# A decoder trunk: state tiles worked on in pairs, with 32-row products in alternate row groups

## The reference

```python
bu_r = jnp.einsum('bsgc,gpc->bsgp', ug, bb_r)      # 16 groups, 16 channels -> 64 states
bu_i = jnp.einsum('bsgc,gpc->bsgp', ug, bb_i)
_, _, h_r, h_i = lax.associative_scan(_cplx_combine, (a_r, a_i, bu_r, bu_i), axis=1)
y = (jnp.einsum('bsgp,gcp->bsgc', h_r, c_re) - jnp.einsum('bsgp,gcp->bsgc', h_i, c_im)
     + d.reshape(SSM_GROUPS, SSM_CH) * ug)
```

## Time and profile before

| | us |
|---|---|
| median of 3 runs | 1702.06 (1700.05 to 1702.82) |
| profiled execution, its own time | 1703.64 |
| span of that execution | 1701.5 |
| PE busy | 1655.4 (97%) |
| DVE busy | 1356.3 (80%) |
| ACT busy | 1084.3 (64%) |
| POOL busy | 225.5 (13%) |

### The profile page before, as it was taken

One profiled execution on the slowest core, in us unless ns is written; L12 is line 12 of the kernel. 1 busy time (PEld: TensorE's weight loads), 2 busy tenths in 40 slices (PEclk: granted clock), 3 DMA queues, 4 the chain that ended last, 5 costly groups with the idle time before them and its releaser, 6 DMA issues.

```text
span 1701.5 us, 24284 instructions
## 1 busy us (share of the span) xinstructions
PE 1655.4 (97%) x8488; PEld 1384.4 (81%) x8488; DVE 1356.3 (80%) x1519; ACT 1084.3 (64%) x1202; POOL 225.5 (13%) x236
## 2 busy tenths in 40 slices
PE   7899999999999999899999999999999999999997
PEld 7778888888897889788888888888888888888785
DVE  6986656555678765679988988988988989889897
ACT  5355544445545554367777777777777777777775
POOL 6643001003703400040000000000000000000200
PEclk9899999999999999999999999999999999999999
DMA  9401435855540144379999999999999999999994
GB/s 379 166 28 73 178 120 223 336 196 179 191 174 22 57 149 169 114 301 393 372 384 373 374 380 379 371 394 377 372 379 372 384 381 360 385 381 361 408 385 171
DMA packets 68213, 475.97 MB, mean 280 GB/s; under 512 B 8011, under 2 KB 8145, under 8 KB 13492
## 3 DMA queue, kind: packets, MB, share of 16 engines
q1 hardware_dynamic: 62044, 450.41, 69.2%
q0 software_dynamic: 5728, 24.05, 3.6%
q10 hardware_dynamic: 376, 0.64, 0.1%
HBM read 463.00 MB, written 13.25 MB: 280 GB/s over the span
## 4 chain that ended last, share of the span: by engine, by line
PE 79%; issue 8%; DVE 7%; ACT 3%; DMA 1%; POOL 1%; DVEq 0%; POOLq 0%; SPq 0%; ACTq 0%
PE bank L471 23%; PE bank L473 23%; PE bank L472 23%; DVE lower L495 2%; PE bank L683 1%; ACT upper L491 1%; PE bank L1433 1%; ACT upper L514 1%; DVE xel L1087 1%; PE bank L1650 1%; PE bank L1469 1%; DMA ring<-in_weights 1%; PE bank L1609 1%; DVE row L2003 1%; PE bank L1538 1%
## 5 line engine op out<-in xcount | busy, mean ns | idle before, releaser
L520 DVE TENSOR_TENSOR lower<-ring,upper 128x2048 fp32r<-128x2048 f32 x368 | 846.9, 2302 | 144.1 <-ACT upper L514 131.2
L514 ACT ACTIVATE upper<-ring 128x2048 fp32r<-128x2048 f32 x369 | 706.3, 1914 | 115.2 <-PE bank L473 103.3
L471 PE MATMUL bank<-upper,xeu 128*128 128x512 f32 x896 | 359.8, 402 | 2.7 <-DVE lower L520 2.6
L473 PE MATMUL bank<-upper,xel 128*128 128x512 f32 x896 | 350.5, 391 | 0.0
L472 PE MATMUL bank<-lower,xeu 128*128 128x512 f32 x896 | 349.5, 390 | 0.0
L471 PE MATMUL bank<-upper,htu 128*128 128x512 f32 x536 | 209.6, 391 | 1.6 <-DVE htl L1103 1.6
L473 PE MATMUL bank<-upper,htl 128*128 128x512 f32 x536 | 208.8, 390 | 0.0
L472 PE MATMUL bank<-lower,htu 128*128 128x512 f32 x536 | 208.7, 389 | 0.0
L473 PEld LDWEIGHTS bank<-upper,xel 128*128 128x128 f32 x896 | 168.2, 188 | 35.9
L471 PEld LDWEIGHTS bank<-upper,xeu 128*128 128x128 f32 x896 | 168.3, 188 | 35.4 <-DVE lower L520 3.9
L472 PEld LDWEIGHTS bank<-lower,xeu 128*128 128x128 f32 x896 | 168.7, 188 | 31.7
(11 more groups left out here) (409 smaller groups left out, 2576.8 us busy)
## 6 DMA issues: line engine op xcount, KB each, us to landing
ring<-in_weights SPq DMA_DIRECT2D x423, 1024.0 KB, 6.7
routed_rows<-g POOLq DMA_DIRECT2D x1, 4096.0 KB, 36.7
lp<-in_lparams POOLq DMA_DIRECT2D x1, 3634.5 KB, 14.3
lp<-in_lparams SPq DMA_DIRECT2D x1, 3584.0 KB, 15.0
memraw<-routed_rows POOLq DMA_DIRECT2D x7, 512.0 KB, 8.3
expert_rows<-xk POOLq DMA_DIRECT2D x7, 512.0 KB, 9.2
skewed_bias<-bias_rows POOLq DMA_DIRECT2D x1, 1152.0 KB, 15.4
h<-in_x SPq DMA_DIRECT2D x1, 1024.0 KB, 5.3
```

Source lines behind the costliest of these rows:

```text
L471: pe.matmul(to, x_up, w_up, start=start, stop=False, skip_group_check=True)
L473: return pe.matmul(to, x_lo, w_up, start=False, stop=stop, skip_group_check=True)
L514: act.activation(upper[:, third(q), :], ring[:, q % RING, :], ACT.Copy).then_inc(done, 1)
L520: dve.tensor_tensor(lower[:, q % RING, :], ring[:, q % RING, :], f32(upper[:, third(q), :]), ALU.subtract).then_inc(done, 1)
```

## The change

State tiles are handled two at a time. The input product reads only the 32 rows that hold the tile's channels, and the matmuls of the two tiles alternate, so that neighbours lie in different row groups. The output products alternate in the same way between two column groups of `yb`. The schedule on PE and DVE follows: inputs 0 and 1 behind the compressor, outputs 0 and 1 behind sc, inputs 2 to 7 in iterations 1, 4 and 8 of the loop, and outputs 2 to 7 in iterations 4, 8 and 12.

```diff
-for _n, _e in (("cqT", "act"), ("ckvT", "act"), ("kwT", "act"), ("hid", "dve"), ("bu0", "dve"), ("qn0", "act"), ("qr0", "dve"),
-               ("qn1", "act"), ("qr1", "dve"), ("bu1", "dve"), ("kn0", "act"), ("kn1", "act"), ("kn2", "act"), ("vm0", "act"),
-               ("vm1", "act"), ("kcv", "dve"), ("bu2", "dve"), ("qT0", "act"), ("qT1", "act"), ("qT2", "act"), ("sc", "dve"),
+for _n, _e in (("cqT", "act"), ("ckvT", "act"), ("kwT", "act"), ("hid", "dve"), ("bu0", "dve"), ("bu1", "dve"), ("qn0", "act"), ("qr0", "dve"),
+               ("qn1", "act"), ("qr1", "dve"), ("kn0", "act"), ("kn1", "act"), ("kn2", "act"), ("vm0", "act"),
+               ("vm1", "act"), ("kcv", "dve"), ("qT0", "act"), ("qT1", "act"), ("qT2", "act"), ("sc", "dve"),
-STATES = {1: 3, 3: 4, 5: 5, 7: 6, 9: 7}
-STATES_OUT = {0: 2, 4: 3, 6: 4, 8: 5, 11: 6, 13: 7}
+STATES = {1: (2, 3), 4: (4, 5), 8: (6, 7)}
+STATES_OUT = {4: (2, 3), 8: (4, 5), 12: (6, 7)}
...
-                def state_inputs(j):
-                    name = f"bu{j}"
-                    wait_free(pe, l, name)
+                def state_inputs(pair):
+                    for j in pair:
+                        wait_free(pe, l, f"bu{j}")
                     for c in range(2):
-                        ins = mm(bank(name)[:, c * T:(c + 1) * T], bt[:, j, c, :], uT[:, j // 4, :], start=True, stop=True)
-                    finish(name, ins)
+                        for j in pair:
+                            x = slice(32 * (j % 4), 32 * (j % 4) + 32)
+                            ins = mm(bank(f"bu{j}")[:, c * T:(c + 1) * T], bt[x, j, c, :], uT[x, j // 4, :], start=True, stop=True)
+                            if c == 1:
+                                finish(f"bu{j}", ins)
+                def state_outputs(pair):
+                    pe.wait_ge(state_ready[l], pair[-1] + 1)
+                    for c in range(2):
+                        for j in pair:
+                            y = yb[32 * (j % 4):32 * (j % 4) + 32, (j // 4) * T:(j // 4 + 1) * T]
+                            ins = mm(y, cp[:, c, j, :], state[j % 4][:, c, :], start=(c == 0), stop=(c == 1))
+                            if c == 1:
+                                ins.then_inc(g_free[l], 1)
...
-                state_inputs(0)
+                state_inputs((0, 1))
...
-                state_inputs(1)
...
-                state_inputs(2)
-                pe.wait_ge(ct_ready[l], 1)
-                state_outputs(0)
...
-                state_outputs(1)
+                pe.wait_ge(ct_ready[l], 1)
+                state_outputs((0, 1))
...
                 states(0)
+                states(1)
                 for t in range(TT):
                     settled(("hid", "qr0")[t])
...
-                states(1)
                 wait_tile(dve, l, "kcv")
...
-                states(2)
...
-                    if i in STATES:
-                        states(STATES[i])
+                    for j in STATES.get(i, ()):
+                        states(j)
```

More of the change, by code:

```diff
@@ L133 @@
         _job(f"mk{MEMK[_i]}", "act", 7 + MEMK[_i])
-    if _i in STATES:
-        _job(f"bu{STATES[_i]}", "dve")
+    for _j in STATES.get(_i, ()):
+        _job(f"bu{_j}", "dve")
     _job(f"pT{_i}", "act")
```

## The result

The changed kernel takes 1725.89 us, median of 5 runs (1724.55 to 1737.3); the kernel before took 1701.83 in the runs made beside it (1700.05 to 1702.82). The ratio is 1.0154, 95% interval 1.0136 to 1.0171: slower by some 24 us. The forecast was 1720, range 1701 to 1729. The profiled execution took 1725.67 us, with a span of 1723.6 (before: 1701.5).

The account below looks back on a forecast made before the run. At first sight PE bounds the head loop, with 8.7 us of slack on DVE; the change moves the chain to DVE and ACT. +8.0 in each layer, 16.0, on 1703.6 (1719.6) or the median (1718.1), +2 clock: 1720 us, range 1701 to 1729.

Parts of the forecast that it names:

- A pair costs one on PE: PE: a pair of state products takes the time of one, inputs 1.07 us and outputs 1.08.
- PE's 4.8 us a layer end in waits: Head loop: PE has 4.8 us less to do per layer, and that saving ends in its waits.
- Prelude: Before the first scores: PE waits some 4 us for DVE's rotation before kn2; first scores 97.5 instead of 96.00, +1.5 us.
- the allowance: Prelude, DVE: 0.3 us on top of 4.40, because POOL's work on state 0 begins at the same moment.
- The second state of a pair: DVE: a state right behind another takes 4.40 us, between 3.31 (no stretch) and 5.5 (scans caught as well).
- Loop: Layer 0 head loop: late masked scores delay ACT, DVE and PE; `group_outputs(1)` at 154.5 instead of 146.49, +8.0 us.
- The clock: Both layers together: +2 us, from prelude clock falls against layer 1's slow spell going; ends -1.5 and +9.
- PE stays the bound: Rival, 12%: DVE's extra work finds gaps in the loop and PE's saving counts, 1695.5 us.
- The pairs don't overlap: Rival, 8%: a pair on PE costs 0.86 us more, +1.9 a layer, 1724 us.
- The clock falls repeatedly: Rival, 7%: loop waits of 2 to 3 us add slow clock on top, 1728 us.
- the forecast's case: 66%: DVE's second states delay the loop's chain, 8.0 us a layer, with 1709 to 1729 us.
- The sum: Whole kernel: +8.0 in each of two layers, 16.0, and +2 for the clock, forecast 1720 us.

Follow-up runs that it names:

- the outputs alone: The kernel before with output products of two state tiles alternating between column groups, inputs and DVE's order unchanged: 1694.31 us, ratio 0.9955.
- Holding POOL back: The changed kernel, with POOL beginning the first state of a pair only when DVE has scanned both: 1724.61 us, ratio 1.0135.
- 32 rows, unpaired: The kernel before, with each state's input product reading 32 rows instead of 128, single and in the old order: 1705.04 us, ratio 1.002.
- the next kernel: Holding POOL back, with outputs of states 2 and 3 in iteration 5 instead of 4, of 6 and 7 in 13 instead of 12: 1714.11 us.
- First scores 1.3 us earlier: The outputs alone, with outputs of states 0 and 1 in iteration 0 of the loop instead of ahead of the first scores: 1699.57 us, ratio 0.9985.
- the best one: The kernel before with only the outputs of two state tiles paired, inputs and DVE's order unchanged: 1694.31 us, ratio 0.9955.

## Why the prediction was right, point by point

- *A pair costs one on PE* (1.07 and 1.08 forecast): right. Inputs 1.06, outputs 0.99 by the start of what follows, at full clock. The scores of the earlier trace rows were the right row to go by.
- *PE's 4.8 us a layer end in waits*: right. PE busy 43.93 of 50.50. Where nothing is moved on DVE such a saving counts: the outputs alone take 4 x 1.08 us a layer off PE, 8.6 in all, and the kernel is 7.7 us faster (part of that, as said there, is the clock's).
- *Prelude*: the wait before kn2 was put at some 4 us and is 3.93. First scores forecast +1.5, measured +4.5 counted from A. The mechanism is right. Its own terms add to 97.3 us, not 97.5. Missing are 0.6 (second state 5.26 us here, not 4.7 with the allowance) and 2.4 at half clock (1.97 + 2.93 for 0.9 + 1.5 us of kn2 and vm), which the forecast kept in its clock term. In layer 1 the wait is 4.75 us and the half clock costs 2.2.
- *The second state of a pair* (4.40; bounds 3.31 and 5.5): this is the term of the sum that was mis-sized. It takes 5.30: the scans are caught as well, which the prediction had as its upper bound. The nearest row had POOL's work begin 1.3 us ahead of it (118.97 against 120.30), so that only the adds fell into it. The kernel before has a row that shows more, which the prediction did not use: state 2 in the prelude (90.11), with POOL at work from 89.64, has its scans stretched too (DVE's timeline, adds and scans):

```profile
91.44 1.84 DVE L2003 TENSOR_TENSOR lp<-lp 128x256 f32<-128x256 f32 x2
93.32 1.68 DVE L2185 TENSOR_TENSOR_SCAN lp<-small,lp 128x256 f32<-128x256 f32 x2
```

  Holding POOL back brought 3.3, so the cause is shown. The Trainium skill, "SBUF — State Buffer", section "SBUF: two separate sides", says that VectorE operations with two SBUF inputs and GpSimd operations take a shared pair of ports in turns, each for a whole instruction; the trace agrees (adds 0.76 to 1.87, scans 1.28 to 2.18, and the multiplications that read a bank unchanged at 1.26).
- *Loop*: `group_outputs(1)` forecast 6.5 us later counted from the first scores, measured 8.6 (156.98 - 97.91 against 146.49 - 96.00). Three second states at 0.9 more would be 2.7; 2.1 is what came. The steps between are the forecast's but for one: ACT waits for masked 5 (7.46 us, forecast about 7), `outputs(2)` and `outputs(6)` wait. mk1 is 5.9 later counted from the first scores (forecast 4.4), but not by the forecast's step. That had it wait, PE idle, for bu5's bank; the bank was free at 126.3, and what held mk1 to 127.80 was PE's own queue, busy and in part at half clock. And from 138.31 to 153.95 the page's chain is on PE, where the forecast had DVE's states 6 and 7; DVE's own steps there take what it said (states 6 and 7 8.6 us, forecast 7.7), so the two run nearly level.
- *The clock* (+2, from a fall in the preludes against the spell of layer 1 gone): both came. The preludes lost 2.4 and 2.2; from layer 1's first scores to its first pT bank it was 7.6 us before and is 4.9 now. Sum +1.9. That this is so near the +2 is luck, since the forecast chose its figure between bounds of -1.5 and +9 and worked out no sum. In the loop the clock fell behind both waits of each layer; that is partly beside DVE's chain, and not separated.
- *The rivals.* "PE stays the bound" was to be decided by DVE reaching masked 5 before about 109 us; it got there at 114.44. "The pairs don't overlap" is refuted, although its 1724 is near the time. "The clock falls repeatedly" (1728) is in part what came: behind both loop waits, in both layers. What that costs the kernel is not separated, so the forecast's case and this rival are not fully told apart.
- *The sum*: 16.0 + 2 forecast. The span has 22.1: 16.0, and 5.3 for the longer second states (0.55 in a prelude, 2.1 in a loop, twice), 1.9 of clock, -2.6 at the start and +1.2 behind, which makes 21.8. The last two were in no step, and both are open. The 2.1 is what the loop of layer 0 was longer than forecast, put down to the second states as a whole; layer 1's loop fits it (+6.2, and 2.7 for the spell that is gone, against 6.5 + 2.1).

## What to carry to other kernels

Where two engines are both near the path, price a change by the place of each instruction in its queue, not by the sums: 4.3 us a layer less on PE were worth -7.7 us with DVE's order kept, and 4.8 less in the loop came with +24 when DVE's order was changed too. Pairing two products also doubles the banks that they fill at one time; look at who gets the second bank next, and when it is read (waits of 2.08 and 1.83 us a layer with the reading put off by an iteration, none for mk1 in the changed kernel). And an operation that reads two SBUF operands is not a fixed price: ask what GpSimd does at that moment.

## What the runs showed that I had not expected

- A 32-row product at the lower clock delays the return to full clock: 7.6 to 8.9 us for a stretch that 128 rows pass in 6.1 to 7.2, though PE's record shows it busy 4.00 of 4.00 in both. The one pair of kernels that differs in nothing else (before and "32 rows, unpaired") has 6.8 and 8.0.
- The clock falls without an idle gap, and reproducibly: 0.50 from 532 to 536 us in both profiles of the kernel before, with PE busy 4.00. The Trainium skill, "TensorE: Matmul & The Clock Gate" (Why this matters for your kernels), speaks of idle gaps; the waits of 3.93 and 3.06 us agree, these spells and the 12 us after a wait of 2.79 (none in the next kernel) don't follow from it.
- First scores 1.3 us earlier made the kernel 5 us slower than the best one: a wait of 1.67 us behind them, at a clock of 0.85, then 0.50.
